# Mean square of the gated scan output: the two tiles' squares added on VectorE ahead of one ones-product placed behind the scan

## Chip, cores and metric

One core of one Trainium2 chip. The metric is the device time of one execution in microseconds, lower is better; runs of one kernel are compared by their median.

## What is computed

One layer of a decoder trunk on 1024 tokens of width 1024, float32 throughout: a Mamba-2 mixer and behind it a mixture of experts (4 groups of 8 experts, the best group, then its best two).

The part that matters here, for each of the mixer's 8 channel groups (256 channels, 4 heads of 64, state of 128) and for each of the 8 chunks of 128 tokens:

```python
y = (y_diag + y_off) + xs * d_skip            # chunked scan: within the chunk, and from the carried state
yg = y * silu(z)
yg = yg * rsqrt(mean(yg * yg, over the group's 256 channels) + 1e-6) * norm_w
h  = h + yg @ w_out[the group's 256 rows]
```

Then `u = rms_norm(h)`, the router's logits of `u`, and the experts' gated MLPs.

## The kernel before

**Tiling.** Channels of a group lie in partitions as two tiles of 128, tokens in the free dimension. All products that need accuracy are made of three: an operand is split into a high part in float32r and a low part (`wh`/`wl`, `uTh`/`uTl`, `yh`/`yl`, `woh`/`wol`), and `mm3` issues low x high, high x low, high x high (L1283 to L1285). A plain float32 matmul stands in the trace as two records.

**Order of the work.** Each engine has its own program, written out by hand; engines meet at semaphores alone, and an engine executes its instructions in order. The groups are a loop over two groups at a time (six groups), then the seventh and the last written out (`groups`). In a group the loop `for c in range(1, 9)` handles, in step `c`, the chunk `k = c - 1` that was scanned in the step before (gate, squares, normalisation, output projection) and scans chunk `c`. Step 8 scans the first chunk of the next group. `PLAN` puts two units of the next input projection (24 products `proj` each) into steps 1, 3, 5 and 7 and one into steps 2, 4, 6 and 8: the first ahead of the transposes, the second (`b`) behind `project_out`, in step 1 ahead of it.

*TensorE* in step c: unit, `tcb` (transposes of chunk c + 1 and C times B, L1328, L1329), `sum_squares` of chunk k (two ones-products, L1362, into column 0 of `out_ps[0]`), `scan` of chunk c (`y_ps` L1338 and L1342, `st_ps` L1349), `project_out` of chunk k (12 records: first the half j = 1 after `ylo_done`, then j = 0, which waits for `ms_done` since it overwrites the bank in which the sum of squares lies), unit b, `turn_y` (two transposes of the scan's result, L1355).

*VectorE* in step c: `gate` (`ygf`, L1081 and L1085, waits for `turn_y` of the chunk), the convolution of unit b, `sub_e` (L1019), `gated_low` (`yl`, L1090), the end of unit b (L1011), `prep` of chunk c + 1 (`xdt` L1037, `cbm` L1040, `xds` L1045; waits for ScalarE's copy `btok`), `mean_square` (`ms`, L1095), `y_and_state` of chunk c (`ysb` L1060 and L1062, state L1071 and L1073; L1058 and L1068 in step 8), `make_m` (L1052), the convolution of the unit (L995, L999), the row additions `add_h` (L1104).

*ScalarE* in step c: `gated` (squares `sq` of both tiles in one instruction, L711, then `yh` of both, L713), tanh of unit b, exp of `E`, copies of projections (L678), `btok` (L705), high parts of the next weight pieces (L634, L722). *GpSimd*: low parts of the weight pieces (`wl`, `wol`, L548), and `rstd = ms ** -0.5` (L589). *SyncE* issues the loads of weight pieces, of `E` and, in the last group, of the first experts.

**The last group** has almost no units. TensorE instead transposes `h` rows that are complete (`turn_h`, `proj<-ident,hacc`, L1472; the first half stands ahead of `tcb`, the second behind the scan) and makes the router's logits (L1488) behind `turn_y`; ScalarE copies each half (`turned_h`, the first ahead of `gated`), VectorE normalises rows (L1273), reads logits (from L1217 on) and in steps 5 and 6 chooses experts (L1226 to L1238) between `mean_square` and `y_and_state`. Its last chunks are in `last_chunks`.

The expert stage follows; it begins with a gather of rows (L1806) that needs all routes.

Of the kernel before, what the change touches and what calls it, by code (L numbers as in the profile page):

```python
# [19 lines left out]
ALU = mybir.AluOpType  # L20
# [119 lines left out]
def mamba(nc, hacc, rt, weights, xg, spare, x, norm_w, w_in, conv_w, conv_b, dt_bias, a_log, d_skip, y_norm, w_out, acum_dram,  # L140
# [3 lines left out]
    NT = T // P  # L144
# [7 lines left out]
    with ExitStack() as ctx:  # L152
# [3 lines left out]
        def sem(name):  # L156
            return ctx.enter_context(nc.semaphore(name))
# [126 lines left out]
        yT_done = sem("yT_done")  # L284
        gate_steps = sem("gate_steps")
        sq_done = sem("sq_done")
        yhi_done = sem("yhi_done")
        ylo_done = sem("ylo_done")
        stat_mm = sem("stat_mm")
# [104 lines left out]
        def y_high(G, k):  # L394
            return yh_last if is_last(G) and k == NT - 1 else yh
# [484 lines left out]
        def _(dve):  # L880
# [170 lines left out]
                cb = cbm[:].unsqueeze(1).to_broadcast([P, R, P])  # L1051
                vec.tensor_tensor(E[:, c % 2], E[:, c % 2], cb, ALU.mult).then_inc(m_done, 1)  # L1052

            def y_and_state(G, c):
                wait(dve, y_mm, G, NT, c + 1)
                wait(dve, yT_done, G, NT, c)
                if c % NT == 0:
                    vec.tensor_copy(ysb[:], y_ps[:, 1, :]).then_inc(y_steps, 1)  # L1058
                else:
                    vec.tensor_tensor(heads(ysb[:]), heads(y_ps[:, 0, :]), spread(eac, G, c), ALU.mult).then_inc(y_steps, 1)  # L1060
                    wait(dve, y_steps, G, 2 * NT - 1, sums(c) + 1)
                    vec.tensor_tensor(ysb[:], ysb[:], y_ps[:, 1, :], ALU.add).then_inc(y_steps, 1)  # L1062
                if c == NT - 1:
                    return
                new = S[:, (c + 1) % 2, :]
                wait(dve, st_mm, G, NT - 1, states(c + 1))
                if c % NT == 0:
                    vec.tensor_copy(new, st_ps[:, 0, :]).then_inc(s_steps, 1)  # L1068
                    return
                wait(dve, s_steps, G, 2 * NT - 3, updates(c))  # L1070
                vec.tensor_tensor(heads(new), heads(S[:, c % 2, :]), spread(dch, G, c), ALU.mult).then_inc(s_steps, 1)  # L1071
                wait(dve, s_steps, G, 2 * NT - 3, updates(c) + 1)
                vec.tensor_tensor(new, new, st_ps[:, 0, :], ALU.add).then_inc(s_steps, 1)  # L1073
# [13 lines left out]
            def gated_low(G, k):  # L1087
                wait(dve, yhi_done, G, 2 * NT, 2 * k + 2)
                for t in range(2):
                    vec.scalar_tensor_tensor(y_low(G, k)[:, t, :], ygf[:, t, :], nw[:, bass.ds(val(G, 2, t), 1)],  # L1090
                                             y_high(G, k)[:, t, :].bitcast(F32), ALU.mult, ALU.subtract).then_inc(ylo_done, 1)

            def mean_square(G, k):
                wait(dve, stat_mm, G, NT, k + 1)
# [32 lines left out]
            def body(G):  # L1127
                plan, early, late = steps(G)
                last = is_last(G)
                prev_b = None  # L1130
                for c in range(1, 9):
                    k = c - 1
                    if last and c >= NT - 1:
                        break
                    gate(G, k)
                    if prev_b is not None and prev_b[1] < 8:
                        conv_unit(*prev_b)
                    if not last:
                        sub_e(G, c + 1)
                    gated_low(G, k)  # L1140
                    if prev_b is not None:
                        final_unit(*prev_b, (G[1] + 1) % 2)
                    prep(G, c + 1)
                    mean_square(G, k)
                    logit_tile(router_tile(last, c, 3))
                    if last and c in (5, 6):
                        choose(2 * c - 10, 2 * c - 8)
                    y_and_state(G, c)
                    mean_square_h(router_tile(last, c, 2))
                    make_m(G, c + 1)  # L1150
                    U = unit_of(G, plan[c][0]) if plan[c] else None
                    if U and U[1] < 8:
                        conv_unit(*U)
                    add_h(G, k, 0)
                    if U:
                        final_unit(*U, U[0][1] % 2)
                    norm_h(router_tile(last, c, 2))
                    add_h(G, k, 1)
                    b = unit_b(plan, c)
                    prev_b = unit_of(G, b) if b is not None else None  # L1160

            def last_chunks(G):

                gate(G, NT - 2)
                y_and_state(G, NT - 1)
                gated_low(G, NT - 2)
                mean_square(G, NT - 2)
                wait(dve, ylo_done, G, 2 * NT, 2 * (NT - 1))
                gate(G, NT - 1)
                mean_square_h(NT - 3)  # L1170
                logit_tile(NT - 4)
                add_h(G, NT - 2, 0)
                gated_low(G, NT - 1)
                add_h(G, NT - 2, 1)
                mean_square(G, NT - 1)
                norm_h(NT - 3)
                add_h(G, NT - 1, 0)
                mean_square_h(NT - 2)
                add_h(G, NT - 1, 1)
                logit_tile(NT - 3)  # L1180
                choose(LATE_A, SPLIT)
                norm_h(NT - 2)
                mean_square_h(NT - 1)
                logit_tile(NT - 2)
                place(0, SPLIT)
                logit_tile(NT - 1)
                choose(SPLIT, NT)
                norm_h(NT - 1)
                place(SPLIT, NT)
                vec.tensor_tensor(rt.second[:], e8[:, :, 1], e8[:, :, 0], ALU.subtract).then_inc(counted, 1)  # L1190
                dve.wait_ge(lg_done, NT)
                vec.tensor_tensor(rt.gexp[:], rt.lg[:, :, 0:EG], g8[:, :, 0:1].to_broadcast([P, NT, EG]), ALU.subtract
                                  ).then_inc(less_done, 1)
                dve.wait_ge(tab_mm, 1)
                vec.tensor_scalar(rt.ridx[:, 0:NE], out_ps[1][:, 0:NE], PADROW, None, ALU.add).then_inc(ridx_done, 1)
                dve.wait_ge(count_mm, 1)
                vec.tensor_copy(rt.counts[:], y_ps[:, 1, 0:NE]).then_inc(counted, 1)
                dve.wait_ge(counted, 2)
# [82 lines left out]
        def _(pe):  # L1281
# [75 lines left out]

            def sum_squares(G, k):

                wait(pe, sq_done, G, NT, k + 1)  # L1360
                for t in range(2):
                    mm = nc.tensor.matmul(mean_square_place(G, k), sq[:, t, :], ones[:, 0:1], start=(t == 0), stop=(t == 1))  # L1362
                mm.then_inc(stat_mm, 1)

            def project_out(G, k):
                wait(pe, ylo_done, G, 2 * NT, 2 * k + 2)
# [71 lines left out]
            def body(G):  # L1438
                plan, early, late = steps(G)
                last = is_last(G)  # L1440
                for c in range(1, 9):
# [3 lines left out]
                        unit(*unit_of(G, plan[c][0]))  # L1445
                    turn_h(router_tile(last, c, 2), 0)
                    tcb(G, c + 1)
                    sum_squares(G, c - 1)
                    scan(G, c)
                    b = unit_b(plan, c)  # L1450
                    if b is not None and c == 1:
                        unit(*unit_of(G, b))
# [751 lines left out]
```

## Time and profile before

| | |
|---|---|
| median of 3 runs | 1646.09 us (1642.89, 1646.09, 1646.17) |
| the profiled execution | 1641.32 us, of which the span from the first to the last instruction is 1639.6 us |
| mean granted TensorE clock | 0.983 of 2.4 GHz |
| TensorE (PE) matmul busy | 1566.1 us, 96% |
| weight loads (PEld) | 1268.6 us, 77% |
| VectorE (DVE) | 1264.3 us, 77% |
| ScalarE (ACT) | 713.6 us, 44% |
| GpSimd (POOL) | 607.3 us, 37% |

Setup takes until about 110 us, the eight groups until about 980, the routes until 1006, the experts the rest. Times in the rows below are microseconds from the first instruction, unless marked ns. `out<-ones,sq` names what an instruction writes and reads. A number in brackets at the end of a row is the time in which the engine sat idle before it, and the instruction that released it. TensorE's matmuls overlap in the records, so the weight loads (PEld) show its order more sharply.

### The profile page before, as it was taken

The page shows a single profiled execution, that of the slowest core. Times are in us where ns is not written, and L with a number is a line of the kernel's source. Part 1 is how long each engine was busy: PE and PEld are TensorE (multiplying, and loading weights), DVE is VectorE, ACT ScalarE, POOL GpSimd, SP SyncE. Part 2 cuts the span into 40 slices and gives each one's busy share as a digit, 9 for nine tenths or more (in the row PEclk, how much of TensorE's full clock was granted, in tenths as well). Part 3 has the DMA queues.
Part 4 walks back from the last instruction along what each step waited for, and adds up shares of the span by engine and source line. Part 5 has one row for each costly group of instructions (what it writes and reads, how often), then busy time and mean ns, then how long its engine had stood idle before and what let it go on. Part 6 is the DMA issues. An engine that isn't in the chain of part 4 may idle for free. (4 is left out here: it accounts for less than half of the span.)

```text
span 1639.6 us, 26389 instructions
## 1 busy us (share of the span) xinstructions
PE 1566.1 (96%) x7516; PEld 1268.6 (77%) x7516; DVE 1264.3 (77%) x2300; ACT 713.6 (44%) x1219; POOL 607.3 (37%) x746
## 2 busy tenths in 40 slices
PE   6899999999999999999999886999999999999996
PEld 5788888878888788888888775777777777777774
DVE  6668868768778688688687685888887888888883
ACT  5333222232333232332322442656656666666652
POOL 2221131131230321321311311355666656666664
PEclk9999999999999999999999996999999999999998
DMA  4122121221121221212211665799999999999992
GB/s 157 39 75 59 46 84 33 59 73 46 43 74 39 60 72 46 71 45 58 69 35 40 225 207 228 258 364 354 386 370 377 376 380 372 370 382 372 380 352 68
DMA packets 143298, 292.73 MB, mean 179 GB/s; under 512 B 21644, under 2 KB 72252, under 8 KB 143200
## 3 DMA queue, kind: packets, MB, share of 16 engines
q1 hardware_dynamic: 128208, 266.29, 46.3%
q0 software_dynamic: 14992, 25.22, 4.2%
q8 instruction: 51, 0.84, 0.2%
q14 instruction: 47, 0.39, 0.1%
HBM read 291.81 MB, written 25.30 MB: 193 GB/s over the span
## 5 line engine op out<-in xcount | busy, mean ns | idle before, releaser
L2007 DVE TENSOR_TENSOR gu_lo<-w_gu,gu_hi 128x1024 fp32r<-128x1024 f32 x256 | 306.9, 1223 | 53.6 <-ACT gu_hi L1850 42.9
L1283 PE MATMUL proj<-uTh,wl 128*128 128x512 f32 x768 | 308.6, 402 | 4.5 <-issue 4.3
L1285 PE MATMUL proj<-uTh,wh 128*128 128x512 f32 x768 | 301.0, 392 | 0.0
L1284 PE MATMUL proj<-uTl,wh 128*128 128x512 f32 x768 | 300.1, 391 | 0.0
L1850 ACT ACTIVATE gu_hi<-w_gu 128x1024 fp32r<-128x1024 f32 x256 | 261.2, 1053 | 61.2 <-PE g_ps L1921 36.7
L548 POOL TENSOR_TENSOR wl<-raw,wh 128x512 fp32r<-128x512 f32 x96 | 129.1, 1362 | 387.3 <-ACT wh L634 387.3
L1283 PEld LDWEIGHTS proj<-uTh,wl 128*128 128x128 f32 x768 | 144.9, 189 | 34.4 <-issue 5.0
L1285 PEld LDWEIGHTS proj<-uTh,wh 128*128 128x128 f32 x768 | 144.7, 188 | 31.7
L687 ACT ACTIVATE xbc<-v 128x512 f32<-128x512 f32 x64 | 40.5, 633 | 292.4 <-DVE v L999 292.4
L1284 PEld LDWEIGHTS proj<-uTl,wh 128*128 128x128 f32 x768 | 145.0, 189 | 28.9
L999 DVE SCALAR_TENSOR_TENSOR v<-xr,cw,v 128x512 f32<-128x512 f32 x192 | 146.1, 761 | 14.7 <-DVE v L999 0.5
L589 POOL TENSOR_TENSOR rstd<-ms,mhalf 128x1 f32<-128x1 f32 x64 | 41.3, 646 | 278.9 <-DVE ms L1095 278.9
L1104 DVE SCALAR_TENSOR_TENSOR hacc<-out,rstd,hacc 128x512 f32<-128x512 f32 x128 | 95.4, 745 | 40.3 <-PE out L1285 34.0
L1950 PE MATMUL y<-w_d,hT 128*128 128x512 f32 x256 | 115.0, 592 | 0.0
L1283 PE MATMUL out<-woh,yl 128*128 128x512 f32 x252 | 110.3, 438 | 3.9 <-POOL wol L548 3.5
L711 ACT ACTIVATE sq<-ygf 128x256 f32<-128x256 f32 x64 | 26.7, 417 | 189.6 <-DVE ygf L1085 189.6
L1919 PE MATMUL g_ps<-gu_hi,xTl 128*128 128x512 f32 x256 | 103.7, 405 | 4.8 <-DVE gu_lo L2007 3.4
L1284 PE MATMUL out<-wol,yh 128*128 128x512 f32 x252 | 100.6, 399 | 0.0
L1920 PE MATMUL g_ps<-gu_lo,xTh 128*128 128x512 f32 x256 | 100.6, 393 | 0.0
L1921 PE MATMUL g_ps<-gu_hi,xTh 128*128 128x512 f32 x256 | 100.5, 393 | 0.0
L1285 PE MATMUL out<-woh,yh 128*128 128x512 f32 x252 | 100.5, 399 | 0.0
L1921 PE MATMUL u_ps<-gu_hi,xTh 128*128 128x512 f32 x256 | 100.3, 392 | 0.0
(281 smaller groups left out, 3283.7 us busy)
## 6 DMA issues: line engine op xcount, KB each, us to landing
w_gu<-in_moe_w_gate_dram SPq DMA_DIRECT2D x128, 512.0 KB, 17.5
w_gu<-in_moe_w_up_dram SPq DMA_DIRECT2D x128, 512.0 KB, 17.5
w_d<-in_moe_w_down_dram SPq DMA_DIRECT2D x128, 512.0 KB, 17.4
raw<-in_ssd_w_in_dram SPq DMA_DIRECT2D x96, 256.0 KB, 3.5
E<-acum_dram SPq DMA_DIRECT2D x64, 256.0 KB, 3.5
raw<-in_ssd_w_out_dram SPq DMA_DIRECT2D x32, 256.0 KB, 2.9
hacc<-in_x_dram SPq DMA_DIRECT2D x8, 512.0 KB, 7.5
out_dram<-hacc SPq DMA_DIRECT2D x8, 512.0 KB, 3.9
```

Source lines behind the costliest of these rows:

```text
L548: return nc.gpsimd.tensor_tensor(dst, src, hi.bitcast(F32), ALU.subtract)
L999: vec.scalar_tensor_tensor(v[:], xr[:, half, k:k + HALF], w(k), v[:], ALU.mult, ALU.add).then_inc(conv_steps, 1)
L1104: vec.scalar_tensor_tensor(h, out_ps[j][:], rstd[:, k % 2:k % 2 + 1], h, ALU.mult, ALU.add).then_inc(h_steps, 1)
L1283: nc.tensor.matmul(out, al, bh, start=start, stop=False)
L1284: nc.tensor.matmul(out, ah, bl, start=False, stop=False)
L1285: return nc.tensor.matmul(out, ah, bh, start=False, stop=stop)
L1850: nc.scalar.activation(wh[:, j % RING, :], weights.gate_up(b, j), ACT.Copy).then_inc(w_hi, 1)
L1919: nc.tensor.matmul(ps[:], xTl[:, b, k, :], wh[:, j % RING, f], start=(k == 0), stop=False)
L1920: nc.tensor.matmul(ps[:], xTh[:, b, k, :], wl[:, j % RING, f], start=False, stop=False)
L1921: mm = nc.tensor.matmul(ps[:], xTh[:, b, k, :], wh[:, j % RING, f], start=False, stop=(k == KD - 1))
L1950: mm = nc.tensor.matmul(y_ps[j][:], hT[:, b, k - DS, :], weights.d[b][:, k, cols], start=False, stop=(k == KF - 1))
L2007: vec.tensor_tensor(wl[:, j % RING, :], weights.gate_up(b, j), wh[:, j % RING, :].bitcast(F32), ALU.subtract).then_inc(w_lo, 1)
```

## The change

VectorE gets a new instruction, `add_squares`, behind `gated_low`: it adds the two tiles' squares in place, and `sum_squares` waits for it and makes one ones-product of the sum in place of two. In the seven groups ahead of the last, `sum_squares` moves behind `scan` in TensorE's order, and `mean_square` moves on VectorE from behind `prep` into `y_and_state`, behind its two `ysb` operations and ahead of the state's update. In the last group both keep their places.

```diff
--- before.py
+++ after.py
@@ -284,6 +284,7 @@
         yT_done = sem("yT_done")
         gate_steps = sem("gate_steps")
         sq_done = sem("sq_done")
+        sq_added = sem("sq_added")
         yhi_done = sem("yhi_done")
         ylo_done = sem("ylo_done")
         stat_mm = sem("stat_mm")
@@ -1051,7 +1052,7 @@
                 cb = cbm[:].unsqueeze(1).to_broadcast([P, R, P])
                 vec.tensor_tensor(E[:, c % 2], E[:, c % 2], cb, ALU.mult).then_inc(m_done, 1)
 
-            def y_and_state(G, c):
+            def y_and_state(G, c, squares_of=None):
                 wait(dve, y_mm, G, NT, c + 1)
                 wait(dve, yT_done, G, NT, c)
                 if c % NT == 0:
@@ -1060,6 +1061,8 @@
                     vec.tensor_tensor(heads(ysb[:]), heads(y_ps[:, 0, :]), spread(eac, G, c), ALU.mult).then_inc(y_steps, 1)
                     wait(dve, y_steps, G, 2 * NT - 1, sums(c) + 1)
                     vec.tensor_tensor(ysb[:], ysb[:], y_ps[:, 1, :], ALU.add).then_inc(y_steps, 1)
+                if squares_of is not None:
+                    mean_square(G, squares_of)
                 if c == NT - 1:
                     return
                 new = S[:, (c + 1) % 2, :]
@@ -1089,6 +1092,11 @@
                 for t in range(2):
                     vec.scalar_tensor_tensor(y_low(G, k)[:, t, :], ygf[:, t, :], nw[:, bass.ds(val(G, 2, t), 1)],
                                              y_high(G, k)[:, t, :].bitcast(F32), ALU.mult, ALU.subtract).then_inc(ylo_done, 1)
+
+            def add_squares(G, k):
+
+                wait(dve, sq_done, G, NT, k + 1)
+                vec.tensor_tensor(sq[:, 0, :], sq[:, 0, :], sq[:, 1, :], ALU.add).then_inc(sq_added, 1)
 
             def mean_square(G, k):
                 wait(dve, stat_mm, G, NT, k + 1)
@@ -1138,14 +1146,16 @@
                     if not last:
                         sub_e(G, c + 1)
                     gated_low(G, k)
+                    add_squares(G, k)
                     if prev_b is not None:
                         final_unit(*prev_b, (G[1] + 1) % 2)
                     prep(G, c + 1)
-                    mean_square(G, k)
+                    if last:
+                        mean_square(G, k)
                     logit_tile(router_tile(last, c, 3))
                     if last and c in (5, 6):
                         choose(2 * c - 10, 2 * c - 8)
-                    y_and_state(G, c)
+                    y_and_state(G, c, None if last else k)
                     mean_square_h(router_tile(last, c, 2))
                     make_m(G, c + 1)
                     U = unit_of(G, plan[c][0]) if plan[c] else None
@@ -1164,6 +1174,7 @@
                 gate(G, NT - 2)
                 y_and_state(G, NT - 1)
                 gated_low(G, NT - 2)
+                add_squares(G, NT - 2)
                 mean_square(G, NT - 2)
                 wait(dve, ylo_done, G, 2 * NT, 2 * (NT - 1))
                 gate(G, NT - 1)
@@ -1171,6 +1182,7 @@
                 logit_tile(NT - 4)
                 add_h(G, NT - 2, 0)
                 gated_low(G, NT - 1)
+                add_squares(G, NT - 1)
                 add_h(G, NT - 2, 1)
                 mean_square(G, NT - 1)
                 norm_h(NT - 3)
@@ -1357,10 +1369,8 @@
 
             def sum_squares(G, k):
 
-                wait(pe, sq_done, G, NT, k + 1)
-                for t in range(2):
-                    mm = nc.tensor.matmul(mean_square_place(G, k), sq[:, t, :], ones[:, 0:1], start=(t == 0), stop=(t == 1))
-                mm.then_inc(stat_mm, 1)
+                wait(pe, sq_added, G, NT, k + 1)
+                nc.tensor.matmul(mean_square_place(G, k), sq[:, 0, :], ones[:, 0:1], start=True, stop=True).then_inc(stat_mm, 1)
 
             def project_out(G, k):
                 wait(pe, ylo_done, G, 2 * NT, 2 * k + 2)
@@ -1445,8 +1455,11 @@
                         unit(*unit_of(G, plan[c][0]))
                     turn_h(router_tile(last, c, 2), 0)
                     tcb(G, c + 1)
-                    sum_squares(G, c - 1)
+                    if last:
+                        sum_squares(G, c - 1)
                     scan(G, c)
+                    if not last:
+                        sum_squares(G, c - 1)
                     b = unit_b(plan, c)
                     if b is not None and c == 1:
                         unit(*unit_of(G, b))
```

## Rows read from the trace of the kernel before

**Rows 1.** Busy time in stretches: us, then each engine's busy us (records), clock

```profile
110.00:980.00 870.00, 848.15 (x4334) 711.15 (x4335) 675.00 (x1559) 274.60 (x640) 202.55 (x195) 1.00 0.24 71
...
1100.00:1200.00 100.00, 100.00 (x439) 77.19 (x439) 80.92 (x87) 65.34 (x82) 62.37 (x86) 1.00 0.97 365
```

**Rows 2.** Waits of TensorE from 1005 us on

```profile
PE tp L1907 <- DMA xg<-u_dram,ridx: 10.5, 1, 10.5
```

**Rows 3.** Waits from 110 to 980 us: in total, times, longest (PEld, DVE)

```profile
PEld out L1362 <- ACT sq L711: 13.8, 20, 1.5
PEld out L1283 <- DVE ms L1095: 3.0, 6, 0.5
DVE ygf L1081 <- PE st_ps L1355: 35.9, 22, 3.5
```

**Rows 4.** Timeline of weight loads, step 5, third group: start us, us, what

```profile
402.64 0.52 PEld L1362 LDWEIGHTS out<-ones,sq 128*128 128x128 f32 x4 [0.63 <-ACT sq L711]
403.08 0.30 PEld L1338 LDWEIGHTS y_ps<-S,xbc 128*128 128x128 f32 x2
...
404.73 0.19 PEld L1283 LDWEIGHTS out<-woh,yl 128*128 128x128 f32 x1
...
406.11 0.19 PEld L1283 LDWEIGHTS out<-woh,yl 128*128 128x128 f32 x1
```

**Rows 5.** Timeline of VectorE, the same step

```profile
403.20 0.61 DVE L1090 SCALAR_TENSOR_TENSOR yl<-ygf,nw,yh 128x128 fp32r<-128x128 f32 x2 [0.28 <-ACT yh L713]
404.55 0.42 DVE L1037 TENSOR_TENSOR xdt<-tcb,dtT 128x256 f32<-128x256 f32 x1 [0.73 <-ACT btok L705]
404.89 0.28 DVE L1040 TENSOR_TENSOR cbm<-tcb,tri 128x128 f32<-128x128 f32 x1
...
405.43 0.15 DVE L1095 TENSOR_SCALAR ms<-out 128x1 f32<-128x1 f32 x1
405.50 0.41 DVE L1060 TENSOR_TENSOR ysb<-y_ps,eac 128x256 f32<-128x256 f32 x1
...
406.29 0.42 DVE L1071 TENSOR_TENSOR S<-S,dch 128x256 f32<-128x256 f32 x1
```

**Rows 6.** Timeline of VectorE, GpSimd and weight loads, step 7 of the same group

```profile
432.53 1.50 DVE L1045 TENSOR_TENSOR xds<-xdt,dst 128x256 f32<-128x256 f32 x1
433.95 0.15 DVE L1095 TENSOR_SCALAR ms<-out 128x1 f32<-128x1 f32 x1
...
432.46 2.72 POOL L548 TENSOR_TENSOR wl<-raw,wh 128x512 fp32r<-128x512 f32 x2 [8.80 <-ACT wh L634]
...
434.15 0.19 PEld L1283 LDWEIGHTS out<-woh,yl 128*128 128x128 f32 x1 [0.51 <-DVE ms L1095]
```

**Rows 7.** Timeline of VectorE and GpSimd, step 6, same group

```profile
421.47 0.42 DVE L1060 TENSOR_TENSOR ysb<-y_ps,eac 128x256 f32<-128x256 f32 x1 [1.03 <-PE y_ps L1342]
...
422.27 0.98 DVE L1071 TENSOR_TENSOR S<-S,dch 128x256 f32<-128x256 f32 x1
...
420.45 2.51 POOL L548 TENSOR_TENSOR wl<-raw,wh 128x512 fp32r<-128x512 f32 x2 [14.24 <-ACT wh L634]
```

**Rows 8.** Timeline of VectorE and weight loads, step 3, same group

```profile
376.67 0.15 DVE L1095 TENSOR_SCALAR ms<-out 128x1 f32<-128x1 f32 x1
...
377.44 0.19 PEld L1283 LDWEIGHTS out<-woh,yl 128*128 128x128 f32 x1
```

**Rows 9.** Timeline of weight loads and VectorE, last group, two steps

```profile
933.73 0.52 PEld L1362 LDWEIGHTS out<-ones,sq 128*128 128x128 f32 x4 [0.63 <-ACT sq L711]
...
941.12 0.62 PEld L1472 LDWEIGHTS proj<-ident,hacc 128*128 128x128 f32 x4
...
942.93 0.52 PEld L1362 LDWEIGHTS out<-ones,sq 128*128 128x128 f32 x4 [0.63 <-ACT sq L711]
...
943.49 0.61 DVE L1090 SCALAR_TENSOR_TENSOR yl<-ygf,nw,yh 128x128 fp32r<-128x128 f32 x2 [1.15 <-ACT yh L713]
```

**Rows 10.** Busy time in stretches of the last group, columns as in rows 1

```profile
918.00:922.00 4.00, 4.00 (x12) 3.10 (x11) 2.04 (x3) 0.46 (x1) 3.09 (x9) 0.57 0.87 224
922.00:926.00 4.00, 2.92 (x23) 2.63 (x22) 2.58 (x8) 2.52 (x6) 0.00 (x0) 1.00 0.95 367
```


## The prediction

> **What bounds the kernel now.** I read the span and the waits first, then one step after another. While the eight groups run (110 to 980 us) TensorE computes for 848 of 870 us [rows 1]; the expert stage behind it starts when the gathered rows land [rows 2] and keeps TensorE busy, for all of the 100 us from 1100 on [rows 1], so a delay of the groups moves the end by its own length. TensorE's weight loader waits for the squares 13.8 us in 20 places, and for VectorE's `ms` 3.0 us in 6 [rows 3]. That looks like a bill which the change removes. It is not, because of what VectorE does at those places.
>
> I call the passes of the loop over `c` steps 1 to 8. In steps 3, 5 and 7 VectorE is behind, without an idle stretch of its own other than those in which it waits for ScalarE. TensorE comes to the squares too early, waits 0.63 us in step 5 [rows 4], and goes on. In steps 4, 6 and 8 it is the other way round: VectorE's `ygf` waits for TensorE's transpose in 22 places, 35.9 us [rows 3]. So the state crosses from one engine to the other once in two steps. An odd step ends its debt at the seventh product of `project_out`, which may not overwrite the bank before `ms` is read, and from there TensorE runs without a gap to the transpose that frees VectorE. Whatever makes that seventh product later is paid in full; whatever makes TensorE faster between a transpose and that product is lost.
>
> **The removed product.** Four records of L1362 take 0.44 us from their first start to the next line's (402.64 to 403.08) [rows 4]; half of them gives 0.22 us a chunk. If all 64 counted that would be 14.1 us.
>
> **The new add.** 128x128 f32, one instruction. The nearest row is `cbm`, the same shape, 0.28 us, of which 0.07 overlaps the next [rows 5]; I take 0.2. The lower end is 0, since in the regular groups it falls into VectorE's wait for `btok` (0.73 us in step 5 [rows 5]). The upper end is 1.50 us: what `xds`, an operation of two SBUF operands of twice the width, takes in step 7 while GpSimd works on `wl` [rows 6], where `S*dch`, also of two SBUF operands and as wide, takes 0.42 in step 5 [rows 5]. GpSimd's pieces start at 432.46 and 420.45 [rows 6, 7], behind the place of the add in those steps, so I stay at 0.2, hidden in the seven regular groups, and on the path in the last.
>
> **Step 5, old and new.** TensorE would reach the scan at 402.01 (402.64 less the wait of 0.63) instead of 403.08. The scan lasts 1.65 us (403.08 to 404.73) [rows 4], to 403.66. There it now waits for the add: `yl` ends at 403.81, the add near 404.0 [rows 5]. Product at 404.05, first `project_out` record 404.3, seventh 1.38 us later (404.73 to 406.11 [rows 4]), 405.7: 0.4 us gained, if nothing else moved. But `ms` moves behind the two `ysb` operations. VectorE's `xdt` still waits for the same `btok`, so `ysb` takes the place of `ms` at 405.43, and what follows `ysb` follows 0.79 us later (405.50 to 406.29 [rows 5]): `ms` at 406.22. The seventh product follows `ms` by 0.20 us, as in step 7 (433.95 to 434.15 [rows 6]): 406.42 against 406.11. Step 5 costs **+0.31 us**.
>
> **Step 3** by the same sum: `ms` stood at 376.67, now 377.46, the product at 377.66 against 377.44 [rows 8]: **+0.22 us**.
>
> **Step 7** has no slack: the seventh product already waits for `ms` (0.51 us [rows 6]). The 0.79 us are paid in full, unless VectorE arrives earlier. It could: in step 6 `ysb` waited 1.03 us for the scan [rows 7], which now comes 0.44 us sooner. But behind `ysb` stands the product `S*dch`, 0.98 us long instead of 0.42, and it ends at 423.25 just behind GpSimd's two pieces (420.45 to 422.96) [rows 7]. Starting 0.4 us sooner it would still start inside the second piece and end where it ends today. With that stretch fixed, step 7 costs **+0.79 us**; if the 0.44 came through, +0.4. The Trainium skill (SBUF — State Buffer, Who interferes with whom) says that a VectorE instruction with two SBUF inputs and a GpSimd one that reads SBUF exclude each other for a whole instruction, and the later one fully blocks. By that rule the step costs the 0.79; if the two merely slowed each other, about 0.4, and the total below would be 2 us less. The row at 422.27 ends right behind the pieces, which agrees with the rule.
>
> **Steps 8, 1, 2, 4, 6.** Steps 8 and 1 have TensorE in front and slack behind: -0.22 us each. What steps 2, 4 and 6 save lies between a transpose and the next debt of VectorE, and is lost. A regular group then comes to -0.44 + 0.22 + 0.31 + 0.79 = +0.88 us. The wait for `ms` is there 6 times [rows 3], in the first six groups: 6 x 0.88 = **+5.3 us**. In the seventh, without that wait, I take 0.
>
> No DMA is issued elsewhere; SyncE's load of `E` waits for the scan, which comes sooner in the regular groups. `rstd` on GpSimd waits behind `ms` and comes up to 0.8 us later; the row additions that need it stand four microseconds later, and the weight pieces behind it in steps 1, 2 and 8 feed units of the next group.
>
> **The last group** keeps the product ahead of the scan, but it waits for the add too. There the loop is: squares' product (933.73), scan, products, logits, transposes of `hacc` at 941.12 (7.39 us later); ScalarE, by the order of its program, copies those and then squares; the next product starts at 942.93, 1.81 us after the transposes [rows 9]. The period is 9.20 us. In the new kernel the product waits not for the squares but for `yl` (943.49 to 944.10 [rows 9]) and the add, so it starts near 944.35, 1.42 us later, and takes 0.22 less: **+1.2 us a step** in steps 2, 3 and 4, 3.6 us. In steps 5 and 6 VectorE chooses experts between `ms` and `ysb` and is the later one: only the add counts, 0.2 each. Behind the loop the squares' product of the seventh chunk stands ahead of the transposes of the eighth. The same 1.4 us between the squares and the end of the add less the 0.22 apply there, of which I take +1.1. The last one is hidden. Sum **+5.1 us**. Ends: 1.0 (only the adds count) and 7 (1.2 in steps 5 and 6 as well).
>
> **Sum.** 5.3 + 0 + 5.1 = +10.4 us. The profiled execution took 1641.3 us and becomes 1651.7. It lay 4.8 us below the median of the three runs, 1646.1, from 1642.9 to 1646.2; I forecast the median, **1656.5 us**. A measurement of this kernel can tell about 0.2%, 3.3 us, from no change.
>
> **Rivals.**
> A, faster: VectorE's odd steps are not what binds, because its chain starts sooner when TensorE does. For it: the waits for the squares are real, 13.8 us [rows 3]. Against it: `xdt` in steps 3, 5 and 7 waits for ScalarE, which hangs on `ygf`, not on TensorE. Its price: 64 x 0.22 = 14.1 us less, of the waits some 6 us kept, and the last group's 5.1 added: -14.1 - 7.8 + 5.1 = -17 us, 1629. Chance 0.09.
> B, little: the seventh product of steps 3 and 5 is late as computed, but the savings of the even steps and the 0.44 of step 6 reach VectorE. Then a group is 0.88 - 3 x 0.22 - 0.4 = -0.2, the last group stays: between +1 and +5, 1649. For it: the 22 waits of `ygf` say that VectorE follows TensorE in the even steps [rows 3]. Against it: the stretch behind GpSimd's pieces. Chance 0.20, of which 0.12 lies within 0.2%.
> C, much slower: in the last group the idle time of TensorE grows from 0.63 to 2 us a step, and its clock falls. From 918 to 922 us the granted clock was 0.57, so mostly its 1.2 GHz level, and 12 records of products filled 4 us [rows 10], where the usual spacing of 1.38/6 = 0.23 us [rows 4] makes it 2.8: 1.2 us lost. A fall in three or four of the last group's steps gives some +4 us on top, 1660. Against it: in the next 4 us TensorE was idle for 1.1 and the clock stood at 2.4 GHz [rows 10]. Chance 0.14.
> Forecast: 0.57.
>
> **Range.** Downwards it takes in most of B and the lower end of the last group, 1647; upwards C and the upper end, 1663. Slower by over 0.2%: 0.57 + 0.14 + 0.08 of B = 0.79. Within: 0.12. Faster: 0.09.
>
> **What would show it.** Right: in the new trace the wait for squares is gone in steps 3 and 5, a wait of `project_out` for `ms` stands in their place, about 0.7 us, 12 times or more, and above 1 us in step 7; L1362's records are 128 (two records a chunk) instead of 256; the group period grows by about 0.9 us; the last group's steps 3 and 4 are 1.2 us longer, with TensorE's loader waiting for the add. Wrong: `ms` is not followed by a late seventh product, or the group's period shrinks; or the S product of step 6 ends sooner.

## The result and the profile after

The changed kernel takes 1662.44 us (median of 4 runs, 1657.68 to 1669.14) against 1646.13 us before (4 runs, 1642.89 to 1647.52). The ratio is 1.0107, with a 95% interval of 1.0077 to 1.0136: slower by 16 to 18 us, where +10.4 was forecast. The median lies just inside the upper end of the range, the ratio times the time before (1663.7 us) just outside. The profiled execution has a span of 1657.3 us, 17.7 more than the 1639.6 before. Of the executions below one stands apart: the kernel of one experiment (`ms` late, and nothing else) once took 2270.26 us at a mean granted clock of 0.652, and that run is left out of its ratio.

The page of the changed kernel: the span and the busy times.

```profile
span 1657.3 us, 26197 instructions
PE 1573.8 (95%) x7388; PEld 1263.6 (76%) x7388; DVE 1271.8 (77%) x2364; ACT 717.0 (43%) x1219; POOL 604.9 (36%) x746
```

TensorE has 128 records fewer (7516 before) and VectorE 64 instructions more, which is the change and nothing else; yet PE is busy for 7.7 us *longer*. Fewer records that take longer fit a lower clock (its mean is 0.974, where it was 0.983), and we come to it. First the waits of the weight loader, from 110 to 980 us, of the changed kernel (in total, times, longest); before they stood in [rows 3].

```profile
PEld out L1295 <- DVE ms L1103: 24.7, 30, 1.4
PEld out L1373 <- DVE sq L1099: 19.8, 23, 2.7
```

The wait for `ms` grew from 3.0 us in 6 places to 24.7 in 30. The wait for the squares did not go away: it is now a wait for the add (`sq`, L1099), 19.8 us instead of 13.8.

To see where the 17.7 us are, I take the start of each chunk's `turn_y` (L1355, now L1367) from the timeline of weight loads. The difference of two starts is the length of a step. Here are the fourth group, the seventh and the last, in us (the first steps of the third and the fifth are disturbed before and after, 18.6 to 19.3 us in place of 16.5 to 16.8):

```
                  step 1    2     3     4     5     6     7     8
4th group before   16.76 11.33 17.32 11.25 17.42 11.26 16.63 10.83
          after    16.49 11.10 17.65 11.38 17.52 11.03 17.68 10.61
7th group before   16.76 11.44 17.19 11.26 17.10 11.25 16.73 10.83
          after    16.49 11.27 17.02 11.02 16.86 11.02 17.00 10.61
last      before   16.48  8.12  9.19  9.19 10.86 11.21  5.42
          after    15.83 10.84 13.60 12.04 11.96 13.60  6.28
```

Over the first six groups the changed kernel loses 4.8 us (from 0.4 to 1.3 a group), over the seventh it gains 1.3, and over the last it loses 13.7. What is left, 0.5 us, lies ahead of the groups and behind them.

**The regular groups** do what the working said. Step 5 of the third group, weight loads and VectorE, answers to [rows 4, 5]:

```profile
404.40 0.30 PEld L1361 LDWEIGHTS st_ps<-xds,btok 128*128 128x128 f32 x2
405.14 0.30 PEld L1373 LDWEIGHTS out<-ones,sq 128*128 128x128 f32 x2 [0.44 <-DVE sq L1099]
405.36 0.19 PEld L1295 LDWEIGHTS out<-woh,yl 128*128 128x128 f32 x1
...
407.50 0.19 PEld L1295 LDWEIGHTS out<-woh,yl 128*128 128x128 f32 x1 [0.91 <-DVE ms L1103]
```

```profile
404.27 0.61 DVE L1093 SCALAR_TENSOR_TENSOR yl<-ygf,nw,yh 128x128 fp32r<-128x128 f32 x2 [0.28 <-ACT yh L714]
404.81 0.28 DVE L1099 TENSOR_TENSOR sq<-sq 128x128 f32<-128x128 f32 x1
405.62 0.42 DVE L1038 TENSOR_TENSOR xdt<-tcb,dtT 128x256 f32<-128x256 f32 x1 [0.53 <-ACT btok L706]
...
406.51 0.42 DVE L1061 TENSOR_TENSOR ysb<-y_ps,eac 128x256 f32<-128x256 f32 x1
406.96 0.42 DVE L1063 TENSOR_TENSOR ysb<-ysb,y_ps 128x256 f32<-128x256 f32 x1
407.30 0.15 DVE L1103 TENSOR_SCALAR ms<-out 128x1 f32<-128x1 f32 x1
```

The scan no longer waits; the product behind it does, 0.44 us, for the add. `ms` follows the start of `ysb` by 0.79 us, and the seventh product follows `ms` by 0.20, after a wait of 0.91 us. The add takes 0.28 us and hides in the wait for `btok`, which shrinks from 0.73 to 0.53.

Step 6 and step 7 of the same group, VectorE and GpSimd and the loader, against [rows 6, 7]:

```profile
422.30 0.42 DVE L1061 TENSOR_TENSOR ysb<-y_ps,eac 128x256 f32<-128x256 f32 x1 [0.55 <-PE y_ps L1354]
...
423.17 1.36 DVE L1074 TENSOR_TENSOR S<-S,dch 128x256 f32<-128x256 f32 x1
...
421.73 2.52 POOL L549 TENSOR_TENSOR wl<-raw,wh 128x512 fp32r<-128x512 f32 x2 [13.54 <-ACT wh L635]
...
436.23 0.19 PEld L1295 LDWEIGHTS out<-woh,yl 128*128 128x128 f32 x1 [1.42 <-DVE ms L1103]
```

`ysb` of step 6 does start earlier (its wait for the scan is 0.55 instead of 1.03 us), and `S*dch` behind it takes 1.36 us instead of 0.98: it ends at 424.53, 0.28 behind GpSimd's two pieces (424.25), as it did before. In two of the kernels tested below it takes 0.75 us (`ms` at its old place) and 0.54 us (the move alone) in this place:

```profile
419.82 0.75 DVE L1074 TENSOR_TENSOR S<-S,dch 128x256 f32<-128x256 f32 x1
```

```profile
421.17 0.54 DVE L1074 TENSOR_TENSOR S<-S,dch 128x256 f32<-128x256 f32 x1
```

Counted from the start of step 6, the end of `S*dch` is at 10.27 to 10.29 us in these two, before the change and after it, however late it starts. The 0.44 us are lost there, and step 7 pays the whole wait for `ms`, 1.42 us instead of 0.51.

**The last group** is another matter. Steps 2 and 3 of it, weight loads, answer to [rows 9]:

```profile
928.20 0.30 PEld L1373 LDWEIGHTS out<-ones,sq 128*128 128x128 f32 x2 [2.71 <-DVE sq L1099]
...
940.16 0.30 PEld L1373 LDWEIGHTS out<-ones,sq 128*128 128x128 f32 x2 [2.06 <-DVE sq L1099]
940.37 0.43 PEld L1350 LDWEIGHTS y_ps<-S,xbc 128*128 128x128 f32 x2
940.89 2.04 PEld L1354 LDWEIGHTS y_ps<-xdt,E 128*128 128x128 f32 x8
```

The wait of 0.63 us became 2.06: 1.43 more, forecast 1.42. But the eight records of the scan that come next take 2.04 us, where in the regular groups they take 1.08. Busy time and clock of stretches of ten us (us, busy us of PE, PEld, DVE, ACT, POOL with records, clock, DMA share, GB/s), first of the changed kernel:

```profile
930.00:940.00 10.00, 8.29 (x45) 7.16 (x44) 6.52 (x15) 3.15 (x8) 1.34 (x2) 0.83 0.82 287
940.00:950.00 10.00, 9.84 (x43) 8.48 (x43) 6.38 (x18) 2.85 (x8) 1.48 (x2) 0.66 0.51 182
950.00:960.00 10.00, 8.13 (x44) 7.12 (x44) 6.18 (x22) 5.08 (x13) 1.48 (x2) 0.83 0.48 142
```

then of the kernel before:

```profile
930.00:940.00 10.00, 9.56 (x68) 8.59 (x67) 8.36 (x24) 4.96 (x13) 1.47 (x2) 1.00 0.88 317
940.00:950.00 10.00, 9.56 (x69) 8.69 (x68) 8.64 (x24) 4.96 (x13) 1.48 (x2) 1.00 0.88 281
```

TensorE got 43 to 45 records done in 10 us instead of 68, at a mean granted clock of 0.66 to 0.83 instead of 1.00. In stretches of one us the clock stands at its lower level, 1.2 GHz, five times between 930 and 985 us, for some 3 to 7 us each; before the change it stood at 1.00 from 922 to 976. That is rival C, much larger than I had priced it.

### The profile page after: what moved, and what is told of

It is laid out like the page before. It is cut to its first block and busy times, and to the rows that moved or that the text cites. A ratio compares the mean times of both kernels' runs of the same rounds, so it can differ in the third digit from the quotient of the medians.

```text
span 1657.3 us, 26197 instructions
## 1 busy us (share of the span) xinstructions
PE 1573.8 (95%) x7388; PEld 1263.6 (76%) x7388; DVE 1271.8 (77%) x2364; ACT 717.0 (43%) x1219; POOL 604.9 (36%) x746
## 5 line engine op out<-in xcount | busy, mean ns | idle before, releaser
L1932 PE MATMUL u_ps<-gu_hi,xTl 128*128 128x512 f32 x256 | 100.3, 392 | 0.0
```

What stands on the lines that cost most here:

```text
L1932: nc.tensor.matmul(ps[:], xTl[:, b, k, :], wh[:, j % RING, f], start=(k == 0), stop=False)
```

## The experiments

The theory to be tested (1): the first seven groups lose by the late `ms`; the last group loses by its longer loop, and as much again because TensorE's clock falls in the longer waits. Its rivals are in the expectations.

### The last group as before

The regular groups of the changed kernel, the last group of the kernel before.

```diff
             def add_squares(G, k):
+                if is_last(G):
+                    return
...
             def sum_squares(G, k):
+                if is_last(G):
+                    wait(pe, sq_done, G, NT, k + 1)
+                    for t in range(2):
+                        mm = nc.tensor.matmul(mean_square_place(G, k), sq[:, t, :], ones[:, 0:1], start=(t == 0), stop=(t == 1))
+                    mm.then_inc(stat_mm, 1)
+                    return
                 wait(pe, sq_added, G, NT, k + 1)
```

> The changed kernel, but the last group has the two ones-products of before, which wait for the squares alone, and no add. The first seven groups keep the change. Theory 1 (the excess over the forecast is made in the last group, where the product waits for the add, and TensorE's clock falls in the idle time): the seven groups give what their trace of the changed kernel gives, +4.8 us for six and -1.3 for the seventh, and the last group is back at its 70.5 us (first to last turn_y): total +3.5 us over the kernel before, 1649 to 1650. Theory 2 (the excess comes from the regular groups, whose delay puts the last group into another phase): the last group stays above 75 us and the total above 1655.

Measured: 1650.05 us against 1645.58, ratio 1.0029 (1.0019 to 1.0040), +3 to +7 us. The last group takes 69.9 us, its steps 2 to 7 within 0.2 us of those of before (8.30, 9.20, 9.19, 10.86, 11.22, 5.42). The rival, which laid the excess on the regular groups, is out. What the groups ahead of the last cost is the small part.

### The change in the last group alone

```diff
             def add_squares(G, k):
+                if not is_last(G):
+                    return
...
-                wait(pe, sq_added, G, NT, k + 1)
+                if not is_last(G):
+                    wait(pe, sq_done, G, NT, k + 1)
...
+                    return
+                pe.wait_ge(sq_added, k + 1)
```

where the line of dots stands for the two products of before, and with `sum_squares` and `mean_square` at their places of before in all groups.

> The kernel before, with the change in the last group alone (add on VectorE, one ones-product that waits for it, places as they were). Theory 1: the last group takes 84 us instead of 70.5, the total is 12 to 15 us above the kernel before, and the granted clock falls to 0.5 five or six times between 925 and 990 us. Theory 2: no more than 5 us above it.

Measured: ratio 1.0101 (1.0059 to 1.0143), median 1665.58 us with one run as low as 1653.23; more than the 12 to 15 us that I expected. In the profiled run the last group takes 89.6 us (84 expected), with steps 2 to 6 of 12.5 to 13.6, and the granted clock is 0.73 to 0.77 from 925 to 985 us:

```profile
925.00:940.00 15.00, 11.54 (x57) 10.14 (x57) 8.17 (x21) 6.32 (x18) 2.17 (x3) 0.77 0.63 236
940.00:955.00 15.00, 12.47 (x60) 11.02 (x61) 9.71 (x31) 6.56 (x18) 1.48 (x2) 0.74 0.55 208
```

Eight products fewer for the whole kernel, and 17 us more by the ratio, 20 by the medians. These runs spread over 13 us and those of the changed kernel over 11, where those of the first experiment spread over 5. The mean granted clock of each run goes with its time: 0.970 in the three runs of 1665.19 to 1666.41 us, 0.981 in the one of 1653.23, which is 8 us above the kernel before. So the same program ran once without most of the falls, and was 12 us faster. How the falls lie can be seen in the profiled execution alone.

### The idle time filled

The changed kernel, with work for TensorE in the last group's wait.

```diff
             def sum_squares(G, k):
+                if is_last(G) and 1 <= k < NT - 2:
+                    for _ in range(8):
+                        nc.tensor.matmul(y_ps[:, 0, 0:P], tri[:], ones[:], start=True, stop=True)
                 wait(pe, sq_added, G, NT, k + 1)
```

> The changed kernel, with eight products of two constant tiles (about 1.8 us) ahead of the wait for the add in steps 2 to 6 of the last group; their result is overwritten, and they fill a time in which TensorE idled 2 us. Theory 1a (of the 13.7 us which the last group lost, about 5 are the longer loop and about 9 the lower clock): the clock stays at 1.0 until the last chunks, steps 3 and 4 take 10.4 us instead of 13.6 and 12.0, and the kernel is 6 to 9 us faster than the changed one. Theory 1b (the loop itself is longer by what is seen, and the clock is a mere companion): no faster than the changed kernel, perhaps slower.

Measured: 1655.12 us (1654.27 to 1656.80), ratio 1.0058 (1.0041 to 1.0075). A kernel that does more work is 7 us faster than the changed one. Steps 2 to 6 of its last group are 9.28, 10.40, 10.41, 11.06 and 11.46 us, against the 8.12, 9.19, 9.19, 10.86 and 11.21 of before: +1.16, +1.21, +1.22, +0.20, +0.25, where 1.2, 1.2, 1.2, 0.2 and 0.2 had been worked out. Windows and one step's weight loads of this kernel:

```profile
940.00:950.00 10.00, 9.91 (x72) 9.05 (x71) 7.76 (x23) 5.08 (x13) 1.47 (x2) 1.00 0.73 274
950.00:960.00 10.00, 9.92 (x72) 9.04 (x70) 7.75 (x23) 5.08 (x13) 1.47 (x2) 1.00 0.76 236
```

```profile
950.83 1.87 PEld L1374 LDWEIGHTS y_ps<-ones,tri 128*128 128x128 f32 x16
952.97 0.30 PEld L1376 LDWEIGHTS out<-ones,sq 128*128 128x128 f32 x2 [0.28 <-DVE sq L1099]
953.19 0.30 PEld L1350 LDWEIGHTS y_ps<-S,xbc 128*128 128x128 f32 x2
953.52 1.08 PEld L1354 LDWEIGHTS y_ps<-xdt,E 128*128 128x128 f32 x8
```

The same wait, filled with 1.87 us of products that nobody reads (the scan overwrites them): the clock stays at 1.00, from 928 to 986 us, and the scan's eight records are back at 1.08 us. The last group takes 76.4 us, 5.9 over before: 4.0 in steps 2 to 6, 1.7 in step 7 and 0.2 in step 1. I call these 5.9 the loop's, and the other 7.8 of the changed kernel's 13.7 the clock's. That is a net figure: the changed kernel loses 9.4 us against this one in steps 2 to 6 and gains 0.8 in each of steps 1 and 7.

### `ms` at its old place

As the first experiment, with `mean_square` ahead of `y_and_state` again.

```diff
                     prep(G, c + 1)
-                    if last:
-                        mean_square(G, k)
+                    mean_square(G, k)
...
-                    y_and_state(G, c, None if last else k)
+                    y_and_state(G, c)
```

> As e1_last_as_before (last group as before the change), with ms at its place of before on VectorE, behind prep and ahead of ysb, in the regular groups; the add and the single product behind the scan stay. Theory 1 (the regular groups lose because ms, behind the two ysb, holds back the seventh product of project_out): steps 3 and 5 each become about 0.4 us shorter than in the kernel before instead of longer, step 7 is no longer than before, a group takes 1 to 1.5 us less than before, and the total is 8 to 10 us under the kernel before, about 1637. Rival (the product behind the scan is itself the delay, or ms now waits for the product on VectorE and delays ysb): within 3 us of e1_last_as_before, or slower.

Measured: 1634.87 us (1634.31 to 1636.93), ratio 0.9940 (0.9923 to 0.9956): **10.7 us faster than the kernel before** and 15.2 faster than the first experiment, from one line. The steps of the profiled executions show somewhat less: the groups together are 7.1 us shorter than before (the profiled execution of the kernel before lies 4 us under its median), and the first six are 12.4 us shorter than in the first experiment. Steps of the fourth group: 16.49, 11.12, 17.13, 11.14, 17.01, 11.03, 16.90, 10.61. Step 5 of the third, loader and VectorE:

```profile
401.94 0.30 PEld L1380 LDWEIGHTS out<-ones,sq 128*128 128x128 f32 x2 [0.76 <-DVE sq L1101]
402.15 0.19 PEld L1296 LDWEIGHTS out<-woh,yl 128*128 128x128 f32 x1
...
403.50 0.19 PEld L1296 LDWEIGHTS out<-woh,yl 128*128 128x128 f32 x1
```

```profile
403.30 0.15 DVE L1105 TENSOR_SCALAR ms<-out 128x1 f32<-128x1 f32 x1
403.37 0.41 DVE L1061 TENSOR_TENSOR ysb<-y_ps,eac 128x256 f32<-128x256 f32 x1
```

The product waits 0.76 us for the add; the first and the seventh product of `project_out` stand nearly at the usual distance (1.35 us, 1.38 before), and the step is 0.4 us shorter than before. Step 7 is 0.27 us longer than before, which I had not expected; but step 6 is 0.23 shorter, and the two together take 27.93 us, where it was 27.89. The `xds` of step 7 is still blocked, and `ms` with it, so what step 6 saves is lost in step 7.

### The move alone

The first experiment's last group, two products of the squares behind the scan, `ms` at its old place, no add.

```diff
-                    sum_squares(G, c - 1)
+                    if last:
+                        sum_squares(G, c - 1)
                     scan(G, c)
+                    if not last:
+                        sum_squares(G, c - 1)
```

> The product moved behind the scan and nothing else, in the regular groups: still two ones-products of the squares, waiting for the squares, no add, ms at its place of before; last group as before. Theory 1 (of the 10.7 us that e4_ms_ahead is under the kernel before, the move gives the end of the waits of steps 3 and 5, and the halving gives 0.22 us in steps 1, 2, 8): steps 1 and 8 as before (16.76 and 10.83 us), step 5 about 0.5 us shorter than before, total 5 to 9 us under the kernel before and 2 to 5 above e4_ms_ahead. Rival (the halved product is what pays): no more than 3 us under the kernel before.

Measured: 1637.82 us against 1645.20, ratio 0.9958 (0.9942 to 0.9975), -7 us. Steps of the fourth group: 16.76, 11.32, 17.01, 11.27, 16.83, 11.27, 16.64, 10.83. Steps 1, 2 and 8 are those of before; steps 3 and 5 are shorter by 0.31 and 0.59 us. So of the gain of the version above some 7 us come from the move and some 3 from the halved product, though the halving gives 0.1 to 0.3 us in steps 1, 2, 4, 6 and 8 and costs 0.1 to 0.3 in 3, 5 and 7. The 3 us are six times the 0.5 of the second, fourth and sixth groups; the intervals of the two ratios overlap.

### The add and the single product without the move

```diff
-                    if last:
-                        sum_squares(G, c - 1)
-                    scan(G, c)
-                    if not last:
-                        sum_squares(G, c - 1)
+                    sum_squares(G, c - 1)
+                    scan(G, c)
```

on the version with `ms` at its old place.

> Add and single product in the regular groups without the move: the product stays ahead of the scan and waits for the add, ms at its place of before; last group as before. Theory 1 (the add is only cheap because the product that waits for it moved behind the scan): in steps 3, 5 and 7 TensorE waits some 1.4 us longer ahead of the scan, each of them is 1 us or more longer than before, the total is 10 to 25 us above the kernel before. Rival (the wait hides under the rest): within 5 us of the kernel before.

Measured: 1689.55 us, ratio 1.0284 (1.0261 to 1.0307), +44 us by the medians and +47 by the ratio, nearly twice the upper end of what I expected. Its waits for the add, 110 to 980 us:

```profile
PEld out L1380 <- DVE sq L1101: 42.9, 27, 2.3
```

Steps 3, 5 and 7 of the fourth group take 20.04, 20.42 and 17.71 us, 2.7, 3.0 and 1.1 over before. The loader waits up to 2.3 us ahead of the scan, not 1.4 more than before as I took, and the granted clock fell to its lower level in twelve stretches between 170 and 790 us, which it never did before in that part. How the time divides between wait and clock was not measured. What was measured is that the add in front of the scan costs more than the halved product can give.

### `ms` late, and nothing else

```diff
                     vec.tensor_tensor(ysb[:], ysb[:], y_ps[:, 1, :], ALU.add).then_inc(y_steps, 1)
+                if squares_of is not None:
+                    mean_square(G, squares_of)
...
-                    mean_square(G, k)
+                    if last:
+                        mean_square(G, k)
```

on the kernel before (two products ahead of the scan).

> The kernel before, with ms behind the two ysb operations in the regular groups and nothing else changed (two products ahead of the scan, no add). Theory 1 (the late ms is the loss of the regular groups): steps 3, 5 and 7 are longer by 0.2, 0.3 and 0.8 us, steps 1, 2 and 8 as before, total 6 to 10 us above the kernel before. Rival (the loss needs the product behind the scan): within 2 us of the kernel before.

Measured: 1652.4 us (median of six runs), ratio 1.0044 (1.0030 to 1.0059), +7 us. Steps of the fourth group: 16.76, 11.33, 17.43, 11.38, 17.49, 11.26, 17.46, 10.83. Steps 3, 4, 5 and 7 are longer by 0.11, 0.13, 0.07 and 0.83 us, the others unchanged. The sum of a group, 1.14 us, is near the 1.3 expected, and it sits in step 7 more than I had thought. Steps 6 and 7 together take 28.72 us, and 28.71 in the changed kernel: there the late `ms` is the whole of the loss.

### `ms` ahead of the blocked `xds`

`ms` at its old place, in step 7 one operation further ahead.

```diff
                 vec.tensor_tensor(cbm[:], tp[:, 3, :], tri[:], ALU.mult).then_inc(cbm_done, 1)
+                if squares_of is not None:
+                    mean_square(G, squares_of)
```

> As e4_ms_ahead, and in step 7 of the regular groups ms stands on VectorE ahead of xds, which is held up there by GpSimd's piece for over 1 us. Theory 1 (the seventh product of project_out waits for ms in step 7 because xds is blocked): its wait for ms goes, step 7 falls from 16.9 to about 16.2 us, total 3 to 5 us under e4_ms_ahead, 1630 to 1632. Rival (ms then waits for the product behind the scan, or VectorE is late in step 8): within 1.5 us of e4_ms_ahead.

Measured: 1633.48 us, ratio 0.9937 (0.9919 to 0.9955). Step 7 falls from 16.90 to 16.69 us, less than half of what I expected, and the totals of this and the version before it can't be told apart. The wait for `ms` is gone in step 7, and a new one stands at the first product of the second unit:

```profile
429.59 0.30 PEld L1384 LDWEIGHTS out<-ones,sq 128*128 128x128 f32 x2 [0.30 <-DVE sq L1103]
432.82 0.19 PEld L1300 LDWEIGHTS proj<-uTh,wl 128*128 128x128 f32 x1 [0.39 <-issue]
```

The profile shows no releaser; by the program that product waits for the other engines to be done with the projection's bank.

### Two products in the odd steps, one in the others

```diff
             def sum_squares(G, k):
+                if k in (2, 4, 6):
+                    wait(pe, sq_done, G, NT, k + 1)
...
+                    return
+                wait(pe, sq_added, G, 5, (0, 1, 3, 5, 7).index(k) + 1)
```

The line of dots stands for the two products again.

> As e6_ms_ahead_xds, but in steps 3, 5 and 7 of the regular groups the product behind the scan is the two ones-products of the squares, which wait for the squares alone, and there is no add; the other steps keep the add and the single product. Theory 1 (in the odd steps VectorE is late, so waiting for the add costs more there than 0.22 us; in the others TensorE is the later one, and the halving pays): steps 3 and 5 as in e5_move_alone (17.0 and 16.84 us), step 7 at 16.3 us, the even ones, 1 and 8 as in e4_ms_ahead; a group 0.6 to 1 us less than e4_ms_ahead, total 1629 to 1631. Rival (step 7 is bound elsewhere): 1632 to 1635.

Measured: 1638.09 us against 1649.28 in the same runs, ratio 0.9945 (0.9925 to 0.9964). A group takes 111.4 us, as in the version with `ms` at its old place (111.4 to 111.5): no gain. Steps 3 and 5 are at 17.24 and 17.08, above the 17.01 and 16.83 of the move alone. The expectation was wrong: the parts don't add up. Steps 2 and 3 together take 28.37 us, 28.33 in the move alone; steps 4 and 5 take 28.22 and 28.10. What the even step saves on TensorE comes back in the odd one, where TensorE waits for `ms` (14 waits, 6.3 us).

### The last group's product behind the scan

```diff
-                    if last:
-                        sum_squares(G, c - 1)
                     scan(G, c)
-                    if not last:
-                        sum_squares(G, c - 1)
+                    sum_squares(G, c - 1)
```

> As e9_mixed, and in the last group the two products stand behind the scan as well (they wait for the squares alone). Theory 1 (in the last group every wait of TensorE ahead of the scan is on its loop, so the wait of 0.63 us a step for the squares is worth something when it is moved behind the scan): steps 3 and 4 of the last group fall from 9.19 to 8.6 to 9.1 us (VectorE's own loop has only some 0.1 us of slack), the total is 0.5 to 2 us under e9_mixed, more if the clock stays up. Rival (ms then comes later on VectorE and holds back the seventh product): no gain, up to 3 us slower than e9_mixed.

Measured: 1640.38 us, ratio 0.9945 (0.9926 to 0.9964), equal to the version above. Steps 3 and 4 of the last group fall from 9.19 to 9.12 us, and step 2 from 8.08 to 7.20, but steps 5 to 7 take 11.56, 13.67 and 7.05 us instead of 10.86, 11.23 and 6.10, in a stretch with a lower clock (0.66 from 950 to 960 us, 1.00 in the version above). Steps 3 and 4 gained 0.07 us where I had expected up to 0.6 and had put VectorE's slack at 0.1; that VectorE sets them is my reading, and no run here isolates it.

## Why the prediction was right and wrong

**Right: the regular groups.** Forecast +0.88 us a group and +5.3 over six, measured +4.8. By parts, of the fourth group: step 1 -0.27 (forecast -0.22), step 8 -0.22 (-0.22), steps 2 and 3 together +0.10 (+0.22), steps 4 and 5 +0.23 (+0.31), steps 6 and 7 +0.82 (+0.79). That makes +0.66 us, not +0.88. That the six together come so near to 5.3 is in part luck: the first and the fifth group lose 1.1 and 1.3 us, 0.5 of it in step 3, where the second and the fourth lose 0.6 and 0.7. The reason given for each part was seen: the seventh product waits for `ms` in the odd steps (30 waits, 0.8 us each on average, and 1.42 us in step 7, where I had asked for more than 1), and the two experiments on `ms` alone, one adding and one removing its delay, move the time by +7 and -15 us. In steps 3 and 5 the wait for the squares did not vanish, as one of my signs had it; it became the wait for the add that the working gives (0.39 us in step 5, measured 0.44). Step 7 was right because `S*dch` of step 6 ends behind GpSimd's piece wherever it starts. By the Trainium skill (SBUF — State Buffer, Who interferes with whom), whose rule I had weighed there, the later instruction blocks fully; the rows of 0.54 to 1.36 us, which all end some 0.28 us behind GpSimd's pieces, agree.

**Wrong by a little: the seventh group.** I took 0; it gained 1.3 us. It has no blocked `xds` in step 7 (0.42 us there, 1.50 in the fourth group) and pays nothing in steps 6 and 7 together (28.02 us, 27.98 before), while steps 1, 2 and 8 gain 0.66 and steps 3 to 5 gain another 0.65. Why steps 3 to 5 gain here and lose elsewhere was not looked into.

**Right: the last group's loop.** +1.2 us in steps 2 to 4 and 0.2 in 5 and 6 were forecast. With the clock held up they measured 1.16, 1.21, 1.22, 0.20 and 0.25. The loop was well worked out: the product waits for the add, and ScalarE copies TensorE's transposes before it squares, which closes the circle. Behind the loop I took +1.1; step 7 measured +1.7.

**Wrong: the step that failed is the price and the chance of rival C**, "A fall in three or four of the last group's steps gives some +4 us on top", at 0.14. The forecast's own sum had nothing for the clock in the last group. The clock was the likely case, not the rival: it fell in the profiled executions of the changed kernel and of the change in the last group alone, and it cost 7.8 us in the former, not 4. I made two mistakes there. First, I priced a fall by twelve products of `project_out`, 1.2 us, and took three or four of them. There were five, and steps 2 to 6 lost 9.4 us by them, 1.9 each. The falls of 7 us take the scan and the `hacc` transposes behind it as well: the scan's eight records alone lose 0.96 us (2.04 against 1.08). The logits' records take 1.86 us in these steps, as before; no fall reached them. Second, I took one stretch of 4 us with 1.1 us of idleness at full clock as evidence against it, while the change was to make a wait of 2 us in every step. The fall in [rows 10], from 918 to 922 us, came right behind a stretch of 4 us in which TensorE had worked for 0.52 us, as the row ahead of it shows:

```profile
914.00:918.00 4.00, 0.52 (x3) 0.35 (x3) 1.85 (x4) 2.45 (x7) 2.96 (x5) 1.00 0.77 165
```

So of the +17.7 us of the span, 4.8 - 1.3 + 5.9 = 9.4 are of the kind I had summed to 10.4, and 7.8 are the clock.

## What to carry to other kernels

An instruction that is moved for the sake of one engine may release another: here reading `ms` frees a bank for the last six of twelve products. Read 0.8 us later on VectorE it cost 15 us (12 by the steps of the six groups), while the move it was meant to accompany gained 7 (5 by the steps). Ask of each moved operation who waits for it, in the step in which that waiter has no slack. And where a change lets TensorE idle in every turn of a loop, price what stands behind the wait at the lower clock level as well (here the scan, the transposes and the products, up to 7 us of a step), and count that case as likely; filling the wait with work that nobody reads is a cheap test.

## What was not expected of the hardware

Sixteen weight loads and products without use, 1.87 us a step, made the kernel 7 us faster, by keeping the granted clock at 1.00 where it had been 0.66 to 0.89. And a VectorE operation of two SBUF operands of 256 elements took 0.42 us by itself and 0.54 to 1.50 us with a GpSimd piece under way; `S*dch` in step 6 then ended 0.28 us behind GpSimd's pieces, whenever it had started. The Trainium skill (TensorE: Matmul & The Clock Gate, Seeing it yourself) shows a clock that goes down behind idle time and comes back under load; the rows here agree in that a wait of 2.06 us a step went with falls, and the same wait filled with products did not.
